# Output projection as three products of rounded parts, and experts ordered by pairs

## What is computed

```python
y = jnp.concatenate([y_gdn, y_diff], axis=-1) @ w_out      # 1024x1024 by 1024x1024
x = layer_norm(alpha * x + g1 * y, ln1_g, ln1_b)
h = modulate(x, sh2, sc2)
# router: best of 4 groups, then the best 2 of its 8 experts, for each token
y_e = (silu(h_e @ w_gate[e]) * (h_e @ w_up[e])) @ w_down[e]    # 1024 -> 512 -> 1024
x = layer_norm(alpha * x + g2 * y_moe, ln2_g, ln2_b)
```

## Time and profile before

| | |
|---|---|
| median of 3 executions | 1810.23 us (1809.44 to 1810.3) |
| profiled execution | 1813.98 us, its span 1812.2 us |
| mean granted TensorE clock | 0.938 of full |
| PE, DVE, ACT, POOL busy | 87%, 53%, 36%, 11% of the span |
| attention | from 767 to 1017 us |
| projection | 1017 to 1176 us |
| routing | 1176 to 1214.7 us |
| experts | 1214.7 to 1746 us |
| combination | 1746 to 1812 us |

### The profile page before, as it was taken

One profiled execution on the slowest core, in us unless ns is written; L12 is line 12 of the kernel. 1 busy time (PEld: TensorE's weight loads), 2 busy tenths in 40 slices (PEclk: granted clock), 3 DMA queues, 4 the chain that ended last, 5 costly groups with the idle time before them and its releaser, 6 DMA issues. The chain is left out here.

```text
span 1812.2 us, 46889 instructions
## 1 busy us (share of the span) xinstructions
PE 1569.8 (87%) x19385; PEld 1084.0 (60%) x19385; DVE 969.2 (53%) x1772; ACT 644.4 (36%) x1639; POOL 199.6 (11%) x269
## 2 busy tenths in 40 slices
PE   5799989999878899869999799729999999996757
PEld 3588866789767888746666455415555555553322
DVE  5798643421054566478888466650404435455636
ACT  4545321121244545346667344212222222221212
POOL 0000000000153453140000000000000000000030
PEclk8899999999978999979999999859999999998979
DMA  8323325531243442130110233175366579999966
GB/s 344 116 70 105 96 83 187 178 133 34 82 121 90 131 128 89 57 132 24 36 47 12 97 131 140 64 278 217 129 247 257 204 288 368 387 396 397 380 218 251
DMA packets 150616, 305.68 MB, mean 169 GB/s; under 512 B 10655, under 2 KB 53103, under 8 KB 147059
## 3 DMA queue, kind: packets, MB, share of 16 engines
q1 hardware_dynamic: 128530, 245.33, 37.8%
q0 software_dynamic: 10336, 46.67, 7.2%
q10 hardware_dynamic: 11520, 10.49, 1.9%
HBM read 256.79 MB, written 45.66 MB: 167 GB/s over the span
## 5 line engine op out<-in xcount | busy, mean ns | idle before, releaser
L2590 PE MATMUL psum<-now_hidden,i_xm 128*32 128x256 f32 x4992 | 309.6, 389 | 26.7 <-DVE now_hidden L2696 25.1
L2590 PEld LDWEIGHTS psum<-now_hidden,i_xm 128*32 128x32 f32 x4992 | 150.8, 111 | 148.9 <-DVE now_hidden L2696 31.5
L2606 PE MATMUL psum<-now_down,i_hT 128*32 128x256 f32 x2464 | 148.9, 382 | 15.0 <-DVE now_down L2695 15.0
L2696 DVE COPY now_hidden<-raw_hidden 128x1024 f32 (+1 forms) x176 | 108.8, 690 | 81.7 <-PE psum L2590 34.9
L2708 DVE TENSOR_TENSOR i_h<-i_silu,psum 128x128 f32<-128x128 f32 x78 | 22.1, 284 | 216.8 <-ACT i_silu L2645 216.8
L2606 PEld LDWEIGHTS psum<-now_down,i_hT 128*32 128x32 f32 x2464 | 79.4, 111 | 71.9 <-DVE now_down L2695 20.4
L2224 PE MATMUL psum<-w_out,g_yT 128*128 128x512 f32 x256 | 115.1, 604 | 8.2 <-ACT g_yT L1787 4.3
L1900 PE MATMUL psum<-dkT,f_qT 64*128 64x512 f32 (+1 forms) x384 | 90.9, 580 | 22.2 <-ACT f_E L1951 19.6
L2695 DVE TENSOR_TENSOR now_down<-raw_down,rep_g 128x1024 f32<-128x1024 f32 x88 | 101.8, 1218 | 9.0 <-PE psum L2606 9.0
L121 PE MATMUL psum<-hT_head,wm_head 128*128 128x512 f32 (+1 forms) x256 | 96.8, 378 | 11.2 <-DVE hT_rest L410 6.9
L1951 ACT ACTIVATE f_E<-psum,f_mx 128x1280 f32<-128x1280 f32 (+2 forms) x96 | 92.1, 969 | 15.0 <-DVE f_mx L2006 15.0
(11 more groups left out here) (356 smaller groups left out, 2895.5 us busy)
## 6 DMA issues: line engine op xcount, KB each, us to landing
raw_hidden<-in_w_gate SPq DMA_DIRECT2D x22, 2048.0 KB, 12.5
raw_hidden<-in_w_up SPq DMA_DIRECT2D x22, 2048.0 KB, 21.2
raw_down<-in_w_down SPq DMA_DIRECT2D x22, 2048.0 KB, 20.4
wa_late<-in_w_ada POOLq DMA_DIRECT2D x16, 1024.0 KB, 5.6
yb<-i_y ACTq DMA_DIRECT2D x80, 128.0 KB, 6.9
wa<-in_w_ada SPq DMA_DIRECT2D x8, 1024.0 KB, 13.5
wt<-in_w_in SPq DMA_DIRECT2D x4, 2048.0 KB, 8.5
wm<-in_w_in SPq DMA_DIRECT2D x12, 512.0 KB, 4.2
```

The source lines that it names most:

```text
L2590: last = nc.tensor.matmul(hidden_bank(s)[j * SUB:(j + 1) * SUB, :], xm[u][:, k, s * SUB:(s + 1) * SUB], now["hidden"][:, :, k, j * P:(j + ...
L2606: last = nc.tensor.matmul(down_bank(s)[j * SUB:(j + 1) * SUB, :], hT[s % 2][:, k * SUB:(k + 1) * SUB], now["down"][:, k, j * WIDE:(j + 1) ...
L2696: return nc.vector.tensor_copy(now[n][:, :, k, :], src)
```

## The change

The output weights are split on chip in a rounded part and the remainder, and so is the transposed tile; a half projection is then 24 rounded products in place of eight f32 ones. The modulation row is no longer multiplied into the weights; DVE multiplies the product with it. Its load, that of the norm rows and of the router's weights move to the start of the projection's stage. DVE's order within a tile changes. The experts are ordered by pairs (largest with smallest, and so on), and the pairs stand alternately from both ends of their list; an odd expert stands last. The loads of the expert at place 1 are issued by the next stage.

```diff
@@ HeadOutputs
+        self.yT_rest = [m.sb(f"g_yT_rest{u}", [P, KD, P], F32R) for u in range(2)]
...
         if t:
             pe.wait_ge(self.kept, t)
+            pe.wait_ge(self.rested, t)
...
+    def keep_rest(self, dve, t):
+        dve.wait_ge(self.kept, t + 1)
+        for g in range(2):
...
+            last = self.m.nc.vector.scalar_tensor_tensor(rest, self.m.bank(g), self.m.keep["nw"][:, g:g + 1], head, ALU.mult, ALU.subtract)
+        last.then_inc(self.rested, 1)
@@ attention
+    HEAD_AT, REST_AT = range(3, 3 + 2 * KD, 2), range(4, 4 + 2 * KD)
...
-            for k in range(KD):
-                w = w_out[:, k, :]
-                nc.gpsimd.tensor_tensor(w, w, rep_mod[:, :], ALU.mult).then_inc(w_scaled, 1)
-            pool.wait_ge(w_scaled, KD)
...
+                if n in HEAD_AT:
+                    if n == HEAD_AT[0]:
+                        act.wait_ge(w_loaded, 32)
+                    k = HEAD_AT.index(n)
+                    nc.scalar.activation(w_head[:, k, :], w_out[:, k, :], ACT.Copy).then_inc(w_headed, 1)
...
+                if n in REST_AT:
+                    k, half = divmod(REST_AT.index(n), 2)
+                    here = slice(half * NC, (half + 1) * NC)
+                    dve.wait_ge(w_headed, k + 1)
+                    nc.vector.tensor_tensor(w_rest[:, k, here], w_out[:, k, here], w_head[:, k, here], ALU.subtract).then_inc(w_rested, 1)
...
+            dve.wait_ge(w_rested, 2 * KD)
+            outputs.keep_rest(dve, 0)
@@ mixed_output
                 if t >= 2:
-                    sp.wait_ge(taken, 2 * t - 2)
+                    sp.wait_ge(stats[0], t - 1)
...
+            sp.dma_start(rep_mod[:, :], d["mod_rows"][2:3, :].to_broadcast([P, D])).then_inc(mod_loaded, 16)
             load_x(0)
+            sp.dma_start(rep_ln[:, :, :], d["rep_ln"].rearrange("p (w n) -> p w n", w=4)[:, 0:2, :]).then_inc(ln_loaded, 16)
+            sp.dma_start(w_route[:, :, :], d["w_route"].rearrange("(k p) n -> p k n", p=P)).then_inc(route_loaded, 16)
...
                 for k in range(KD if t < TL - 1 else KD // 2):
+                    if t == TL - 2 and k == 3:
+                        deviation(0, TL - 1)
...
-                    stt(x1[u][:, here], xt[u][:, here], ALPHA, m.bank(2 + c), ALU.mult, ALU.add).then_inc(taken, 1)
+                    tt(x1[u][:, here], m.bank(2 + c), rep_mod[:, here], ALU.mult).then_inc(taken, 1)
                     dve.wait_ge(taken, 2 * t + c + 1)
+                    link(stt(x1[u][:, here], xt[u][:, here], ALPHA, x1[u][:, here], ALU.mult, ALU.add))
...
             outputs.join(dve, 2)
+            dve.wait_ge(mod_loaded, 16)
             for t in range(TL):
                 add(t)
+                if t + 1 < TL:
+                    outputs.keep_rest(dve, t + 1)
+                if t + 2 < TL:
+                    outputs.mix(dve, t + 2)
+                if t + 3 < TL:
+                    outputs.join(dve, t + 3)
...
                 norm(t)
                 norm_again(t)
-                if t + 2 < TL:
-                    outputs.mix(dve, t + 2)
-                if t + 3 < TL:
-                    outputs.join(dve, t + 3)
...
                 for k in range(KD):
-                    last = nc.tensor.matmul(m.bank(2 + c), yT[t % 2][:, k, :], w_out[:, k, c * NC:(c + 1) * NC],
-                                            start=(k == 0), stop=(k == KD - 1))
+                    for n, w in enumerate((w_head, w_rest)):
+                        nc.tensor.matmul(m.bank(2 + c), yT[t % 2][:, k, :], w[:, k, here], start=(k == 0 and n == 0), stop=False)
+                pe.wait_ge(outputs.rested, t + 1)
+                for k in range(KD):
+                    last = nc.tensor.matmul(m.bank(2 + c), yT_rest[t % 2][:, k, :], w_head[:, k, here], start=False, stop=(k == KD - 1))
@@ routing
             sp.wait_ge(planned, 1)
-            for u in range(2):
-                load_expert(m, sp, u, u)
+            load_expert(m, sp, 0, 0)
...
-            link(ts(last_[:, :], used[:, :], 2.0, -1.0, ALU.mult, ALU.add))
+            link(ts(last_[:, :], used[:, :], -1.0, None, ALU.add))
+            nearest(pairs[:, :], used[:, :], 0.5, -0.25)
+            link(ts(pairs_end[:, :], pairs[:, :], 2.0, -1.0, ALU.mult, ALU.add))
+            link(ts(alone[:, :], pairs[:, :], 2.0, 2.0, ALU.mult, ALU.add))
...
-            link(stt(key[:, :], nth, -2.0, last_[:, :].to_broadcast([P, NE]), ALU.mult, ALU.add))
-            link(stt(pos[:, :], nth, 2.0, key[:, :], ALU.mult, ALU.min))
+            link(ts(key[:, :], nth, -1.0, last_[:, :], ALU.mult, ALU.add))
+            link(tt(pair[:, :], nth, key[:, :], ALU.min))
+            link(tt(second[:, :], nth, pair[:, :], ALU.is_gt))
+            link(ts(key[:, :], pair[:, :], -2.0, pairs_end[:, :], ALU.mult, ALU.add))
+            link(stt(key[:, :], pair[:, :], 2.0, key[:, :], ALU.mult, ALU.min))
+            link(stt(pos[:, :], key[:, :], 2.0, second[:, :], ALU.mult, ALU.add))
+            link(ts(pair[:, :], pair[:, :], pairs[:, :], alone[:, :], ALU.is_ge, ALU.mult))
+            link(tt(pos[:, :], pos[:, :], pair[:, :], ALU.add))
...
-            link(ts(last_[:, :], used[:, :], -1.0, None, ALU.add))
@@ experts
         def _(sp):
+            load_expert(m, sp, 1, 1)
```

More of the change, by code:

```diff
@@ L1725, in __init__ @@
         self.Y = [m.sb(f"g_Y{u}", [P, 2 * H, P]) for u in range(2)]
-        self.sq = m.sb("g_sq", [P, 2 * H, P])
+        self.sq = m.nc.alloc_sbuf_tensor_at("g_sq", [P, 2 * H, P], F32, offset=m.high - 4 * 4 * H * P)
         self.ms = [m.sb(f"g_ms{u}", [P, 2 * H]) for u in range(2)]
-        self.yT = [m.sb(f"g_yT{u}", [P, KD, P]) for u in range(2)]
+        self.yT = [m.sb(f"g_yT{u}", [P, KD, P], F32R) for u in range(2)]
+        self.rest_at = m.top
+        self.yT_rest = [m.sb(f"g_yT_rest{u}", [P, KD, P], F32R) for u in range(2)]
         self.loaded = [m.sem(f"g_loaded{u}", lasting=True) for u in range(2)]
         self.own = m.sem("g_mix_link", lasting=True)
-        self.joined, self.rooted, self.normed, self.turned, self.kept, self.summed = (
-            m.sem("g_" + n, lasting=True) for n in ("joined", "rooted", "normed", "turned", "kept", "summed"))
+        self.joined, self.rooted, self.normed, self.turned, self.kept, self.rested, self.summed = (
+            m.sem("g_" + n, lasting=True) for n in ("joined", "rooted", "normed", "turned", "kept", "rested", "summed"))
         self.linked = 0
@@ L1789, in keep @@
         last.then_inc(self.kept, 1)
+    def keep_rest(self, dve, t):
+        dve.wait_ge(self.kept, t + 1)
+        for g in range(2):
+            here = slice(g * H, (g + 1) * H)
+            head, rest = (y[t % 2][:, here, :].rearrange("p k n -> p (k n)") for y in (self.yT, self.yT_rest))
+            last = self.m.nc.vector.scalar_tensor_tensor(rest, self.m.bank(g), self.m.keep["nw"][:, g:g + 1], head, ALU.mult, ALU.subtract)
+        last.then_inc(self.rested, 1)
 def attention(m):
@@ L1826, in attention @@
     m.keep["nw"] = nw
+    m.keep["outputs_at"] = m.top
     outputs = m.keep["outputs"] = HeadOutputs(m)
-    assert m.top <= HOT
+    assert m.top <= m.high - 4 * 4 * H * P
+    lamr = nc.alloc_sbuf_tensor_at("lamr", [P, 4, DK], F32, offset=outputs.rest_at)
+    lprod = nc.alloc_sbuf_tensor_at("lprod", [P, 2, DK], F32, offset=outputs.rest_at + 4 * 4 * DK)
     lam_loaded, dve_lam, act_lam = m.sem("lam_loaded"), m.sem("lam_dve"), m.sem("lam_act")
@@ L2058, in mixed_output @@
     nc, d, ident, modT = m.nc, m.dram, m.keep["ident"], m.keep["modT"]
-    m.limit = HOT
     raw = m.keep["raw"] = {"hidden": nc.alloc_sbuf_tensor_at("raw_hidden", [P, 2, 2, KD, DE], F32, offset=HOT)}
-    lg, w_out, rep_mod, rep_ln, w_route = (m.keep[n] for n in ("lg", "w_out", "rep_mod", "rep_ln", "w_route"))
+    lg, w_head, w_rest = (m.keep[n] for n in ("lg", "w_out_head", "w_out_rest"))
+    top, m.top, m.limit = m.top, m.high, 229312
+    rep_mod, rep_ln = m.sb("rep_mod", [P, D]), m.sb("rep_ln", [P, 2, D])
+    w_route = m.sb("w_route", [P, KD, NG + NE])
+    m.top, m.limit = top, m.keep["outputs_at"]
+    mod_loaded, ln_loaded, route_loaded = m.sem("g_mod_loaded"), m.sem("g_ln_loaded"), m.sem("g_route_loaded")
     m.scratch("x1", [TL, P, D])
@@ L2069, in mixed_output @@
     outputs = m.keep["outputs"]
-    yT = outputs.yT
+    yT, yT_rest = outputs.yT, outputs.yT_rest
     h2T = twice("h2T", [P, KD, P])
@@ L2145, in _ @@
             for t in range(TL):
-                deviation(0, t)
+                if t < TL - 1:
+                    deviation(0, t)
                 deviation(1, t)
@@ L2241, in route @@
                     pe.wait_ge(lg_kept, t)
+                else:
+                    pe.wait_ge(route_loaded, 16)
                 for k in range(KD):
@@ L2257, in _ @@
             route(TL - 1)
-    m.top = m.after
+    m.top, m.limit = m.after, HOT
 def load_expert(m, sp, place, u, copied=None):
@@ L2304, in routing @@
     v = {n: m.sb("r_" + n, [P, TL]) for n in "gsum e2 den".split()}
```

(4 more changed lines are left out.)

24 lines of the change are left out of this document (10 added, 14 removed).

## The result

| | |
|---|---|
| before, median of 4 | 1809.84 us (1809.36 to 1810.3) |
| after, median of 4 | 1795.56 us (1792.98 to 1798.14) |
| ratio | 0.9912, 95% interval 0.9896 to 0.9929 |
| profiled execution after | 1796.3 us, span 1794.5 us |

The change gains 14.3 us. The forecast was 1789 with a range of 1772 to 1803: the direction and the range hold, the sum promised 21.6 us. The two traces say where the rest is. They are: attention, from its first maximum to the last `f_A`; turn-over, to the statistics of tile 0; tiles, from there to the statistics of tile 7; tail, to the routing stage's first operation; place, to the cast of the order into `plan`; wait, to TensorE's transposes of the first gathered rows; first, to the first mixing product; blocks, from there to the 78th and last.

A forecast was written before the change was run, and what follows sets the result against it. TensorE was taken to bound the projection, SP's load issues the end of routing, TensorE and late weight loads the experts. Terms -5.8 - 7.5 - 6.3 - 2 = -21.6 us gave a forecast of 1789 us, range 1772 to 1803.

The forecast's parts named there:

- Attention: Attention stage: GpSimd's products removed, ScalarE's roundings and two VectorE operations at the end added; -5.8 us, bounds -9 and -1.
- GpSimd's products: Attention stage: removing GpSimd's eight products of the output weights saves 9.6 us, bounds 7 and 10.6.
- ScalarE's roundings and VectorE's differences: Attention stage: eight roundings delay the keep, 0.3 us x 8 = 2.4 us; sixteen differences of 0.68 us stay hidden.
- Projection, tiles: Projection stage: a tile saves 1.1 us, not TensorE's 2.9, so 6.6 us over six steady tiles.
- the loop is 16.9 us: Projection tile: the loop through landed loads, join, norm, deviation, squares and keep takes 16.9 us and sets the tile.
- Projection, first tile and tail: Projection stage: loads moved ahead of tile 2's cost the first tile about +1.6 us; the tail saves some 2.5 us.
- Routing and start: Routing to TensorE's first transposes: moving the second expert's load issues away gains 6.3 us, bounds 3 and 9.
- The order: Experts' stage: ordering by pairs spreads the waits on loads rather than hides them; -2 us, bounds -12 and +6.
- 2,2, 78 in all: Experts' stage: the count of blocks, giving the lightest pair two blocks each and 78 blocks over 22 experts.
- (1): Rival: join finds its data, tile is 15.1 or 15.4 us, the order saves 10 more; 1770 us, chance 0.2.
- (2): Rival: rounding lowers TensorE's time but the tile stays at 18 us, the order costs 4; 1801 us, chance 0.22.
- (3): Rival: TensorE idles in the projection and drops to 1.2 GHz, tile 27 us; 1869 us over eight tiles, chance 0.05.

The follow-up runs named there:

- two_products: Kernel after, without the products of the rounded tile with the remainder of the weights; one execution, 1801.1 us, tiles 114.8 us against 116.0.
- join_behind: Kernel after, with the join of tile t+3 behind the norms again, as it stood before; 1792.6 us, ratio 0.9904.
- two_loads: Kernel after, with the second expert's three loads issued in the routing stage again; 1801.7 us, ratio 0.9958 to the kernel before.

## Why the prediction came out as it did

**Attention: right.** Forecast -5.8. The stretch is 8.2 us shorter, and the remainders of tile 0 behind it cost 1.4 (they stand in the turn-over), so -6.8. Term by term: GpSimd's products -9.9 by the run without them (I took 9.6); ScalarE's roundings and VectorE's differences +1.7 (225.5 against 223.8), where I had 2.4. A head with a rounding takes 6.87 us, one without 6.71: 0.16 and not 0.3, so half of the delay did not reach the next head. The differences stayed hidden.

**Projection, tiles: the mechanism held in part, and the gain was larger.** Forecast -6.6 for the six tiles behind the first. They take 97.4 us in place of 108.1, so -10.7; in the other profiles of the same stage -10.2 to -13.3. What held: TensorE is off the path (two_products), VectorE's own tile is 15.5 us against my 15.4 (join_behind), and in the tile where VectorE stands at the join for 3.09 us, the loads land 6.8 us after the keep (join of 1064.64, keep ended at 1057.86) against 6.4. What failed is "the loop is 16.9 us" as a steady tile. The loads of the tile before it had landed without a wait (join of 1046.27, 5.2 us behind its keep), so only some tiles pay: the waits in the six come to 3.8 us, and the average is 16.2 us, 97.4 / 6.

**Projection, first tile and tail: the first tile twice as dear.** Forecast +1.6 and -2.5. The turn-over is 0.9 longer without the remainders' 1.4, and the first tile takes 18.6 us in place of 16.2, with a join that waits 2.29: +3.3. My sum had a wait for late loads at the stage's start alone; the next join waits too. The tail is 2.0 shorter. The whole projection is -9.4 against -7.5.

**Routing and start: half of the gain missing.** Forecast -6.3 until TensorE's first transposes; measured -2.1 there (place +2.5, wait -4.6) and -3.1 until the first mixing product, a stretch that differs by more than this 1.0 between profiles (11.2 to 12.8). The placing was priced right (2.1 against 2.5), and SP did hold the stage before (two_loads). The step that failed is "next is GpSimd's second gather, issued at 1200.03 + 0.96, now 2.1 later, and a barrier of 1 us". The barrier comes 9.1 us after that issue, not 1: it passes 0.9 us behind the landing of the second gather, 9.2 us after its start, so a gather's landing took SP's place as the bound. My forecast used the 7.7 us for the first gather and forgot the landing of the second. The trace of the kernel before has the same landing, of the second gather of the earlier trace rows:

```profile
i_x<-xn,tok POOLq DMA_INDIRECT x1, 9.1
```

It landed at 1209.1. By the 0.9 us the barrier would have passed at 1210.0, and the stage started at 1214.7, so moving SP's issues away could give no more than 4.7 us; two_loads measured 4.4.

**The order: wrong in sign, by one block.** Forecast -2, measured +5.7 in this pair of profiles; over the eight profiles in this order the blocks take 512.3 to 517.3, so +3 to +8 against 509.1. It is the forecast's own far bound, +6, but not for the reason given there. The step that failed is the count "2,2, 78 in all", and with it the price of the light pair, put at 8.5 like a pair 3,1. It is a pair 2,1, and it costs 17.2 us over its blocks, with waits of 1.89 and 12.96 us for its second load and the next. The prediction's own sum gives this when it is fed three blocks: 3.4 x 6.05 = 20.6 us of compute against 36.0 of loads is a wait of 15.4, where the two waits came to 14.85. With 15.4 for this pair, the sum of the waits is 37.4 and not 30, 6.1 over the 31.3 of before: the waits on the up part were 38.4, the stretch 5.7 us longer. The other prices were good: the pairs 3,1 cost 8.6 and 8.3 against 8.5, although both parts of that sum were too long. From the issue of the load for place 7 (1384.68) VectorE was ready for the copy of place 8 at 1409.56, 24.9 us later against 26.8, and copied at 1418.26, 33.6 us later against 36.0; the errors cancel. In the old order the last pair, 2,1, has no load to cover and costs 2.7 us; the new order gives that place to a pair 5,1, which elsewhere costs 1.4 to 2.1, and puts 2,1 where it has to cover.

The bound in the light pair is the transfers, as the stretch of the longest wait shows; it is the kernel after, and 396 GB/s is the page's rate of full queues:

```profile
1300.00:1326.00 26.00, 14.88 (x202) 7.41 (x201) 12.47 (x17) 2.93 (x9) 0.94 (x1) 0.74 1.05 396
```

Two experts are 12.6 MB, at that rate 31.8 us; three blocks compute for 18, four for 24, five for 30.

**Rivals.** (1) was right of the projection only where the join stands behind the norms; the kernel's 16.2 lies between its 15.4 and the forecast's 16.9. (2) priced the order at +4, nearer than the forecast, but its tile of 18 us is out. (3), slower by the clock, is out too: from 1057.9 to 1122.1 the granted clock was 1.00, and where it was lower (0.96) the tile was among the short ones, 15.2 us. The Trainium skill (TensorE: Matmul & The Clock Gate, Part 1: The HAM clock gate) expects a less busy array to lose its full rate: the trace agrees (0.91 over the stage, 0.84 with a third of the products left out), but it cost nothing there, since another engine sets the tile.

That the time fell into the range was luck in part, for the errors had two signs: attention and projection gave 2.9 us more than forecast (-16.2 against -13.3), the start 3.2 and the order 7.7 less. So -21.6 becomes -13.6, beside the 14.3 of the medians.

## What to carry to other kernels

When an order of work is changed against a limited number of buffers, set for each pair its compute against its loads, and take the counts from an instruction that is made once for each item: one block too many in the lightest pair turned a loss of 6 us into a gain of 2. Ask also which item stands last: what stands there has nothing to cover, so it should be the one that covers least. When the last engine is moved out of the way of a barrier, list everything that the barrier waits for, transfers issued by an engine and not yet landed among it. And where one engine's cover is thin, put an operation that waits on a transfer behind the work that doesn't need it.

## What the runs showed that I had not expected

GpSimd's products slowed VectorE in a definite way. In the timeline of the kernel before, VectorE's operations on one element a partition with two inputs take 2.07 to 2.20 us, nearly as long as one GpSimd product (19.76 / 8 = 2.5 us); beside none they take 0.14 and 0.22:

```profile
790.86 2.07 DVE L2017 SCALAR_TENSOR_TENSOR f_cf<-f_rs,nlam,f_cf 128x1 f32<-128x1 f32 x1
792.96 3.59 DVE L2018 SCALAR_TENSOR_TENSOR f_A<-f_E,f_cf,f_E 128x1280 f32<-128x1280 f32 x1
...
801.22 2.20 DVE L2015 TENSOR_TENSOR f_cf<-f_rs 128x1 f32<-128x1 f32 x1
803.65 2.07 DVE L2017 SCALAR_TENSOR_TENSOR f_cf<-f_rs,nlam,f_cf 128x1 f32<-128x1 f32 x1
...
810.99 0.14 DVE L2015 TENSOR_TENSOR f_cf<-f_rs 128x1 f32<-128x1 f32 x1
811.36 0.22 DVE L2017 SCALAR_TENSOR_TENSOR f_cf<-f_rs,nlam,f_cf 128x1 f32<-128x1 f32 x1
```

The reductions from PSUM between them keep their 0.96 us. The first four rows are 1.85, 2.04, 2.06 and 1.85 us over their usual length (1.55 for `f_A`), and with one more at 789.26 (1.37 us long, 1.23 over) that is 9.0 of the 9.6 us. The Trainium skill (SBUF — State Buffer, Who interferes with whom) says that the two engines share one pair of ports, held for a whole instruction, and that VectorE's operations with two SBUF inputs are touched by a GpSimd instruction that reads SBUF; the trace agrees, and so the price could have been summed from these rows before the change, where I took it from heads with and without.

The second surprise is how late a barrier passes behind a gather (9.1 us of idle GpSimd, until it has landed), and the third that executions of one program differ by 7 us in the start of a stage that no change touched, which is more than most terms here: stretches between two named instructions told apart what medians of the whole time over five or six executions could not.
